# High-half products of two weight tiles between the turns of x, in the opening of a hybrid decoder layer

## What is computed

```
x = x + 0.5 * swiglu(rms_norm(x, g_ffn1), w1_ffn1, w3_ffn1, w2_ffn1)
z = rms_norm(x, g_mix) @ w_in + b_in            # q, k, v, u, vg
... window attention with sinks | gated spatial mixing ...
x = x + concat(attn_out, gm_out) @ w_out + b_out
x = x + 0.5 * swiglu(rms_norm(x, g_ffn2), w1_ffn2, w3_ffn2, w2_ffn2)
x = x + sigmoid(rms_norm(x, g_ple) @ w_ple_gate) * (ple @ w_ple_proj)
y = rms_norm(x, g_final)
```

## Time and profile before

| | |
|---|---|
| Median of 3 runs | 1041.27 us (1041.0 to 1042.39) |
| The profiled execution | 1038.65 us, of it a span of 1036.6 us from first to last instruction |
| TensorE busy | 982.9 us, 95% of the span |
| VectorE, ScalarE, GpSimd busy | 678.0, 455.8, 282.8 us |
| DMA | 101.38 MB, mean 98 GB/s |

### The profile page before, as it was taken

One profiled execution on the slowest core, in us unless ns is written; L12 is line 12 of the kernel. 1 busy time (PEld: TensorE's weight loads), 2 busy tenths in 40 slices (PEclk: granted clock), 3 DMA queues, 4 the chain that ended last, 5 costly groups with the idle time before them and its releaser, 6 DMA issues.

```text
span 1036.6 us, 19264 instructions
## 1 busy us (share of the span) xinstructions
PE 982.9 (95%) x7965; PEld 966.1 (93%) x7965; DVE 678.0 (65%) x997; ACT 455.8 (44%) x742; POOL 282.8 (27%) x157
## 2 busy tenths in 40 slices
PE   6998999999989999999999997999999998999996
PEld 5998999999989998999989997999999998999896
DVE  5888468756648564356784489557756757756475
ACT  6645325533535443565544464424543433535132
POOL 2331111211111126321448413201311111215451
PEclk9998999999999999999999998999999999999998
DMA  7941333252243326321124682143334224234202
GB/s 205 188 98 41 113 112 93 82 151 61 65 122 93 101 74 184 87 62 42 42 61 115 131 165 81 58 137 92 92 92 113 82 62 132 67 111 140 61 22 83
DMA packets 192178, 101.38 MB, mean 98 GB/s; under 512 B 13018, under 2 KB 189492, under 8 KB 192076
## 3 DMA queue, kind: packets, MB, share of 16 engines
q1 hardware_dynamic: 176624, 90.76, 30.8%
q0 software_dynamic: 11440, 5.77, 4.5%
q10 hardware_dynamic: 4028, 3.63, 1.1%
HBM read 97.59 MB, written 3.59 MB: 98 GB/s over the span
## 4 chain that ended last, share of the span: by engine, by line
PE 74%; DVE 10%; ACT 6%; issue 3%; POOL 3%; DMA 3%; SPq 0%; DVEq 0%; ACTq 0%; POOLq 0%
PE ps L1604 40%; PE ps L1684 29%; DMA w_raw<-in_w_ffn_dram 2%; ACT w_hi L687 2%; DVE w_lo L1187 2%; DVE ab L1319 1%; POOL h_lo L1055 1%; PE ps L1640 1%; ACT h_hi L794 1%; DVE x L1334 1%; POOL ssq L1038 1%; ACT xb_hi L699 1%; PE ps L1914 1%; DMA x_rows<-in_x_prompt_dram 1%; DVE ab L1314 1%
## 5 line engine op out<-in xcount | busy, mean ns | idle before, releaser
L1684 PE MATMUL ps<-xo_hi,w_hi 128*128 128x260 f32 x1008 | 286.9, 285 | 11.2 <-ACT snap L766 11.2
L1684 PE MATMUL ps<-xo_lo,w_hi 128*128 128x260 f32 x1008 | 286.9, 285 | 0.0
L1684 PE MATMUL ps<-xo_hi,w_lo 128*128 128x260 f32 x1008 | 286.5, 284 | 0.0
L1604 PE MATMUL ps<-h_hi,w_hi 128*128 128x260 f32 x960 | 197.2, 287 | 17.0 <-DVE w_lo L1187 14.3
L1684 PEld LDWEIGHTS ps<-xo_hi,w_hi 128*128 128x128 f32 x1008 | 192.0, 190 | 11.9 <-DVE w_lo L1282 11.1
L1604 PE MATMUL ps<-h_lo,w_hi 128*128 128x260 f32 x960 | 194.5, 284 | 0.0
L1604 PE MATMUL ps<-h_hi,w_lo 128*128 128x260 f32 x960 | 194.3, 284 | 0.0
L1684 PEld LDWEIGHTS ps<-xo_hi,w_lo 128*128 128x128 f32 x1008 | 192.1, 191 | 0.0
L1684 PEld LDWEIGHTS ps<-xo_lo,w_hi 128*128 128x128 f32 x1008 | 192.1, 191 | 0.0
L1604 PEld LDWEIGHTS ps<-h_hi,w_hi 128*128 128x128 f32 x960 | 149.2, 191 | 19.6 <-DVE w_lo L1187 16.6
L1048 POOL TENSOR_TENSOR w_lo<-w_a,w_hi 128x512 fp32r<-128x512 f32 x36 | 66.0, 1834 | 335.4 <-ACT w_hi L756 335.4
(11 more groups left out here) (253 smaller groups left out, 1451.8 us busy)
## 6 DMA issues: line engine op xcount, KB each, us to landing
w_raw<-in_w_ffn_dram SPq DMA_DIRECT2D x88, 256.0 KB, 3.0
w_a<-in_w_ffn_dram SPq DMA_DIRECT2D x36, 512.0 KB, 5.0
w_raw<-in_w_ffn_dram SPq DMA_DIRECT2D x48, 384.0 KB, 3.5
w_raw<-in_w_ffn_dram SPq DMA_DIRECT2D x16, 512.0 KB, 5.9
w_lo<-in_w_ffn_dram POOLq DMA_DIRECT2D x11, 512.0 KB, 8.7
w_raw<-in_w_in_dram SPq DMA_DIRECT2D x10, 512.0 KB, 3.9
w_raw<-in_w_ple_gate_dram SPq DMA_DIRECT2D x8, 512.0 KB, 3.9
x_rows<-in_x_prompt_dram SPq DMA_DIRECT2D x4, 512.0 KB, 5.6
```

Source lines behind the costliest of these rows:

```text
L1604: ins = pe.matmul(ps[:, bank + step * h, 0:HALF], w[:, c, w0:w0 + P], m_[:, sk, h * HALF:(h + 1) * HALF], start=(first and n == 0), stop=( ...
L1684: ins = pe.matmul(ps[:, b, 0:Q], w[:, c, k * P:(k + 1) * P], m_[:, op, k, :], start=(first and k == 0 and n == 0), stop=(k == 3 and n == 2 ...
```

## The change

The high-half products of up tiles 0 and 1 (hi x hi and hi weight x lo input, four matmuls for each k) are issued between the turns of x: turn m is followed by tile 0's step m - 2 and tile 1's step m - 4 (`first_high`). The low-weight products of the two tiles, 16 matmuls each, follow after all of them (`first_low`), with the turn of the vectors between the two tiles. `first_stat_out` moves into up tile 2, at k = 1. The turns use pairs 2 and 3 by turns, since pairs 0 and 1 now gather the two tiles, and their waits count from m - 2. Up tiles 0 and 1 of the first FFN join `summed`: their low halves come by adding DMA, and GpSimd's two subtractions go. ScalarE's order becomes: squares of the two row blocks, squares of the samples, high half of tile 0, then the loop with tile 1's high half after m = 1, tile 0's negated copy after m = 2 and tile 1's after m = 4.

```diff
-        summed = [("up", 0, n) for n in range(2, N_STD)] + [("up", 1, n) for n in range(3, N_STD)]
+        summed = [("up", 0, n) for n in range(N_STD)] + [("up", 1, n) for n in range(3, N_STD)]
...
+            for b in range(2):
+                act.wait_ge(x_in[b], 16)
+                if b:
+                    act.wait_ge(row_sums, b)
+                nc.scalar.activation(sq_rows[:, 1, :], x_rows[:, b, :], ACT.Square,
+                                     accum_out=rs_t[:, b:b + 1]).then_inc(row_sums, 1)
             act.wait_ge(x_in[NB], 16)
+            act.wait_ge(row_sums, 2)
             nc.scalar.activation(sq_rows[0:TS, 1, :], xs_rows[0:TS, :], ACT.Square,
                                  accum_out=rs_t[0:TS, NB:NB + 1]).then_inc(row_sums, 1)
...
+            high_half(("up", 0, 0))
...
                 if m == 1:
-                    split_hi(("up", 0, 0))
-                elif m == 5:
-                    split_hi(("up", 0, 1))
-
+                    high_half(("up", 0, 1))
+                elif m == 2:
+                    negated(("up", 0, 0))
+                elif m == 4:
+                    negated(("up", 0, 1))
             split_hi(("up", 0, 2))
             ffn_stage(0)
...
-                                between = [(6, lambda: stat_out(2))] if s else [(1, vectors), (5, first_stat_out)]
+                                between = [(6, lambda: stat_out(2))]
+                            elif s == 0:
+                                between = [(1, first_stat_out)]
...
+            def first_high(n, k):
+
+                pe.wait_ge(xg_lo_ready, k + 1)
+                if k == 0:
+                    pe.wait_ge(w_hi_ready, n + 1)
+                c = cell[("up", 0, n)] + k // 4
+                for i, m_ in enumerate((h_hi, h_lo)):
+                    for h in range(2):
+                        pe.matmul(ps[:, 2 * n + h, 0:HALF], wh[:, c, k % 4 * P:(k % 4 + 1) * P],
+                                  m_[:, k, h * HALF:(h + 1) * HALF], start=(k == 0 and i == 0), stop=False)
+
+            def first_low(n):
+
+                lo_wait(pe, ("up", 0, n))
+                for k in range(KD):
+                    c = cell[("up", 0, n)] + k // 4
+                    for h in range(2):
+                        ins = pe.matmul(ps[:, 2 * n + h, 0:HALF], wl[:, c, k % 4 * P:(k % 4 + 1) * P],
+                                        h_hi[:, k, h * HALF:(h + 1) * HALF], start=False, stop=(k == KD - 1))
+                ins.then_inc(unit_done, 1)
+
+            for m in range(KD + 4):
+
+                if m < KD:
+                    if m >= 2:
+                        pe.wait_ge((x_odd, x_even)[m % 2], (m - 2) // 2 + 1)
+                    elif m == 1:
+                        pe.wait_ge(cols_ready, 1)
+                    turn_tile(x_rows, xs_rows, m, 2 + m % 2).then_inc(x_turned, 1)
+                if 2 <= m < KD + 2:
+                    first_high(0, m - 2)
+                if m >= 4:
+                    first_high(1, m - 4)
...
-            ffn_stage(0, turn_vectors)
+            first_low(0)
+            turn_vectors()
+            first_low(1)
+            ffn_stage(0)
```

More of the change, by code:

```diff
@@ L683, in _, with high_half, negated, split_hi @@
         def _(act):
-            def split_hi(key):
+            def high_half(key):
                 act.wait_ge(raw_in[slot[key]], raw[key])
                 nc.scalar.activation(w_at(wh, key), w_at(w_raw, key), ACT.Copy).then_inc(w_hi_ready, 1)
+            def negated(key):
+                act.wait_ge(w_hi_ready, index[key] + 1)
+                nc.scalar.activation(w_at(wl, key), w_at(wh, key).bitcast(F32), ACT.Copy,
+                                     scale=-1.0).then_inc(w_negated, 1)
+            def split_hi(key):
+                high_half(key)
                 if key in summed:
-                    act.wait_ge(w_hi_ready, index[key] + 1)
-                    nc.scalar.activation(w_at(wl, key), w_at(wh, key).bitcast(F32), ACT.Copy,
-                                         scale=-1.0).then_inc(w_negated, 1)
+                    negated(key)
             def x_hi(stat, m):
@@ L829, in _ @@
                     act.wait_ge(x_turned, m + 1)
-                    nc.scalar.activation(x[:, m, 0:TP], ps[:, 2 * (1 + m % 3), :], ACT.Copy)
-                    nc.scalar.activation(x[:, m, TP:T], ps[:, 2 * (1 + m % 3) + 1, 0:TS], ACT.Copy).then_inc(x_odd, 1)
+                    nc.scalar.activation(x[:, m, 0:TP], ps[:, 2 * (2 + m % 2), :], ACT.Copy)
+                    nc.scalar.activation(x[:, m, TP:T], ps[:, 2 * (2 + m % 2) + 1, 0:TS], ACT.Copy).then_inc(x_odd, 1)
                     act.wait_ge(x_odd, m // 2 + 1)
@@ L1731, in first_stat_out, with ffn_stage @@
                 stat_out(0)
-            def ffn_stage(s, vectors=None):
+            def ffn_stage(s):
                 src = xg[2 * s]
@@ L1737, in ffn_stage @@
                         n, = arg
+                        if s == 0 and n < 2:
+                            continue
                         ready, between = None, []
```

15 lines of the change are left out of this document (2 added, 13 removed).

## The result

| | before | changed |
|---|---|---|
| median of 12 runs, us | 1041.04 | 1043.84 |
| lowest to highest, us | 1037.11 to 1043.70 | 1040.87 to 1047.00 |
| profiled execution, us (span) | 1038.65 (1036.6) | 1047.00 (1045.3) |
| ratio to before, 95% interval | | 1.0032, 1.0016 to 1.0048 |

The change makes the kernel slower, by 3.3 us (1.7 to 5.0). The forecast was slower by 6.6 us, 1047.9: the sign is right, the size is twice too large, and the time lies in the range, 0.3 us above its low end.

What follows compares the result with a forecast made beforehand. TensorE, busy 95%, was taken as the bound. The wait at up tile 2 (+3.7), the spread (+1.3) and the fallen clock (+1.6) summed to +6.6 us on a median of 1041.27: 1047.9, range 1043.5 to 1051.5.

Steps and rivals of the forecast that it cites:

- The turns: Turns of x on TensorE: turn 2 waits for ScalarE's eviction until 14.0; turn 7 ends at 25.55 (19.9 before).
- Rival 2: Opening: clock rises with the first products, near 18.7, or does not fall after the wait; say 1046 us; chance 0.17.
- Rival 1: Opening: clock stays at 1.2 GHz while turns and products alternate; +9.8 us, 1051.1; chance 0.28.
- The low half of tile 2: Up tile 2: adding DMA issued at 29.37, TensorE free at 33.9, waiting 3.8 us until 37.7; +3.7 us.
- the landing: Adding DMA of up tile 2: takes 8.3 us from issue, so it lands at 37.7.
- The spread: Spreading of 1/rms (`stat_out`) on TensorE, moved behind the wait at up tile 2: +1.27 us.
- The clock behind the wait: TensorE after the wait at up tile 2: clock falls to 1.2 GHz, 3.2 us at half pace, +1.6 us.
- Rival 3: Up tile 2: TensorE starts it when it did, only the spread is left; +0.8 us, 1042.1; chance 0.13.
- The range: Kernel time from 1043.5 (early clock with a landing of 7.8) to 1051.5 (rival 1).

Runs made afterwards that it cites:

- e12: The changed kernel again, unaltered, for a second profile and more times; 1043.98 us, ratio to before 1.0033.
- e8: The kernel before again, one execution for a second profile; 1040.73 us.
- e6: The kernel before with only the longer list of adding DMAs (low halves of tiles 0 and 1); 1043.29 us, ratio to before 1.0028.
- e1: The changed kernel with the spread of 1/rms ahead of the wait at up tile 2; 1041.54 us, ratio to before 1.0015.
- e3: The changed kernel with each turn waiting for one eviction less, that of the pair it writes; 1042.19 us, ratio to before 1.0032.
- e5: The new order of products alone, low halves of tiles 0 and 1 by GpSimd's subtraction as before; 1045.43 us, ratio to before 1.0043.
- e7: The changed kernel with 18 spare matmuls where TensorE waits for tile 2's low half; 1042.47 us, ratio to before 1.0025.
- e9: The changed kernel with ScalarE making tile 2's high half three times, so its negated copy comes some 2 us later; 1047.53 us, ratio to before 1.0070.
- e11: The kernel before with 11 spare matmuls ahead of the turns; 1044.04 us, ratio to before 1.0030.
- e2: The changed kernel with up tile 2's low half by GpSimd's subtraction instead of adding DMA; 1039.53 us, ratio to before 0.9995.
- e4: The changed kernel with spread ahead of up tile 2, its low half by subtraction, and turns waiting one eviction less; 1038.47 us, ratio 0.9981.

## Where the prediction held, and which step failed

**The turns.** Right to 0.6 us. Turn 2 was forecast for 14.0, with a wait for ScalarE's eviction, and came at 13.61 with it; turn 7 was to end at 25.55 and ended at 25.0. The forecast let the clock rise at 22.1, "the same moment as before"; it rose at 19.3 in this execution and at 22.9 in e12, which is 9.4 and 13.5 us behind the first turn. The 4.1 us make 1.4: the adding DMA of tile 2 is issued 18.9 us behind the first turn in the one and 20.4 in the other, and their openings differ by 1.3. The rest is taken up by waits for ScalarE and VectorE, such as the one at 22.48, which the late clock doesn't have. Rival 2 had priced the early clock in this way, and the first profile is half of it: early clock, but with the fall.

**Rival 1, a slow clock through the alternation,** is excluded in every profile of the new order: the last two turns, which stand between products, took 0.60 to 0.66 us in all of them, and in the changed kernel's first profile from 20.37 on. The rule of the Trainium skill, "TensorE: Matmul & The Clock Gate", "Part 4: PE-mode transpose", that full clock doesn't engage for transposes, is what the earlier trace rows show and what e8 does not: there transposes alone had the clock up at 13.45. In e6, a third profile with all turns together, they stayed at 1.11 us. As a rule for a forecast it is good for "often", not for "never".

**The low half of tile 2.** Issued at 28.82, forecast 29.37; TensorE free at 33.4, forecast 33.9: right to 0.6 us, and they move together, so that the wait hardly feels them.

**The step that failed: the landing.** "I take 8.3, the middle of the two." It was 6.6 us, and 6.4 to 6.5 in every other run of the new order in which this DMA has its place (e1, e3, e5, e7, e12), 7.6 in e9. With 6.6 in place of 8.3 the wait is 33.9 to 36.0, 2.1 us instead of 3.8, and 2.03 was measured; the term of the sum is +2.0 and not +3.7. In the trace it was +1.5 (35.49 against 33.99), since the DMA was also issued 0.55 us earlier than forecast. I argued that the DMAs of tiles 0 and 1 and the loads beside it would lengthen the landing past the 7.8 of the earlier trace rows. They did not: all three adding DMAs of tiles 0 to 2 took 6.6, and e5, with none ahead of tile 2's, has 6.5. On the loads I had the sign wrong, and my own times could have told. The raw load of tile 6 waits until TensorE is done with tile 0. Before, it is issued at 26.95, 1.0 us behind the DMA of tile 2; in the new order tile 0 ends with its low products, and the load comes at 31.46, 2.6 us behind the DMA. The eleven traces in which tile 2 comes by DMA fall in two groups. Where the load follows within 0.5 to 1.1 us (e9, before, e8) the landing took 7.6, 7.8 and 8.3 us; where it follows after 2.1 us or more (e11, then e1, e3, e5, e7, e12 and the changed kernel at 2.6, e6 at 4.9) it took 6.4 to 6.6. This holds without exception, but no run moves the load alone, so it is a pattern and not a shown cause. The next ones took longer, 11.0 (issued at 30.86) and 11.3 (at 35.98), and were hidden in the changed kernel. The earlier trace rows had told that the lengths range from 6.2 to 9.9; a middle is no forecast where the price of the edit hangs on one landing, and I should have carried both ends through the sum: 6.2 gives a wait of 1.7, and a shift near +4.5.

Of the 3.3 us that the forecast was too high, this step explains 2.2: the term was +3.7 and is +1.5 in the trace. The other 1.1 lies between the trace (4.5) and the runs (3.3), inside the interval of the runs.

**The spread.** +1.27, right in the trace: between 35.49 and up tile 3 TensorE takes 8.80 us, 5.77 for the tile as before, 1.27 for the spread and 1.76 for the clock. e1 moves the spread and loses the fall with it; the 1.65 us by which its opening is shorter are for both, less the new wait.

**The clock behind the wait.** Counted in full, +1.6. It fell in the profile after and in e12, and cost 1.8 us in each, and in e5 behind 1.91 us (the spread's long part took 1.91 us there), but not in e3 behind 1.92. That is three of four profiles with a wait of 1.9 to 2.0 us.

With 2.0, 1.27 and 1.6 the sum is 4.9, where the openings grew by 4.3 (the two first profiles) and 5.2 (e12 against e8), and the runs by 3.3 (1.7 to 5.0). The 4.9 and the two openings lie near the upper end of that interval, 5.2 just beyond it. A clock fall that comes in some executions only would lower the mean, by some 0.4 us if the three of four held for all (an estimate from four profiles); the runs without a profile don't show their clock, and so this is argued, and the rest may be no more than the spread of the runs. **Rival 3**, the spread alone (+0.8), is excluded: TensorE did wait, and e2 shows what the kernel is without this wait. (Its +0.8 goes with a start at 33.6, 0.4 us before that of the kernel before; at an equal start it is +1.27.) Of the marks named ahead of the run the wait of 3 to 4.5 us, the start near 37.7 and the shift of 6 to 7 us did not come: they were 2.03, 35.49 and 4.5, all by the landing. The stretch at 1.2 GHz (3.4 us) came, and from up tile 3 to the second product unit the shift does not shrink (4.53, 4.54).

**The range.** That the time lies in it is in part luck. Its low end, 1043.5, was given as the early clock with a landing of 7.8, but the forecast's own times make 1044.9 of these (36.8 less 0.5 is 36.3, so +2.3 and +1.3), above the 1043.84 measured. It takes the shortest landing, 6.2, to come to 1043.3.

The cause, then: the change sends tile 2's low half through 6.6 us of DMA at the one place where the new order leaves 5.7 us less of TensorE's work to hide it (8.4 instead of 14.1). That this wait and what hangs on it is the loss, e2 shows. That the landing is 6.6 here and was 7.8 before goes with the later load of tile 6, untested; where e4's 2 us come from stays open.

## What to carry to other kernels

Where a step is moved, follow the thing that was prepared under it: here the new order was sound, and it lost to an operand that had been hidden with 0.3 us to spare. Ask too which transfers the new order moves closer to it or farther away. A short method on a slow engine (2.4 us on GpSimd) can beat a long one that costs no engine anything (6.6 us of DMA) for the first operand after a reordering; where the operand is needed later, the DMA is hidden and keeps the engine free. And if a wait can't be avoided, put in front of it what is ready: moving one 1.3 us step from behind the wait to ahead of it made the opening 1.65 us shorter.
